# The order of exponentials and probability copies on ScalarE in the steps of NSA attention

## Time and profile before

| what | value |
|---|---|
| runs before | 1071.84 us median of 3 (1071.44 to 1075.18) |
| the profiled execution | 1070.39 us, with a span of 1068.3 us from first to last instruction |
| busy over the span | PE 97%, PEld 81%, DVE 56%, ACT 43%, POOL 12% |
| granted TensorE clock, mean | 0.997 of full speed |
| NSA's steps, from the scores of job 0 to the first product of the next stage | 259.89 to 324.36 us of the span |

### The profile page before, as it was taken

How to read it: one execution, slowest core, us unless ns; L and a number is a source line. 1 busy time by engine, 2 the same in 40 slices (tenths; PEclk the granted TensorE clock), 3 DMA queues, 4 the chain that set the end, 5 groups by cost and what they waited for, 6 DMA issues and landing times.

```text
span 1068.3 us, 13273 instructions
## 1 busy us (share of the span) xinstructions
PE 1033.2 (97%) x5334; PEld 868.8 (81%) x5334; DVE 596.3 (56%) x543; ACT 460.7 (43%) x568; POOL 125.1 (12%) x157
## 2 busy tenths in 40 slices
PE   7999999999999999999999999999997899999997
PEld 6888888889898788898878888888876778888885
DVE  4455543854755754462575544554666884455444
ACT  4555432333773454452434334433436444454430
POOL 1000000232911100000012000000017510000001
PEclk9999999999999999999999999999999999999999
DMA  9656545470311665454447654463522246446531
GB/s 348 220 175 213 206 169 188 138 257 2 110 50 45 234 216 204 166 179 176 158 160 261 218 188 157 158 236 126 209 99 69 90 159 235 157 160 212 179 118 40
DMA packets 78652, 178.51 MB, mean 167 GB/s; under 512 B 2992, under 2 KB 12352, under 8 KB 78608
## 3 DMA queue, kind: packets, MB, share of 16 engines
q1 hardware_dynamic: 76128, 169.16, 45.5%
q0 software_dynamic: 2480, 8.72, 2.5%
HBM read 176.82 MB, written 1.05 MB: 167 GB/s over the span
## 4 chain that ended last, share of the span: by engine, by line
PE 82%; DVE 13%; POOL 3%; ACT 1%; DMA 1%; issue 1%; SPq 0%; POOLq 0%; DVEq 0%; ACTq 0%
PE acc L1193 24%; PE acc L1195 24%; PE acc L1194 24%; DVE w_lo L781 4%; PE trb L1252 4%; PE acc L1396 2%; POOL rstd L480 1%; DVE stats L827 1%; DVE x L835 1%; DVE y L822 1%; PE acc L1375 1%; DMA raw<-ffn_w_gate 1%; DVE neg_max L930 1%; DVE xt_lo L791 1%; PE aux L1445 1%
## 5 line engine op out<-in xcount | busy, mean ns | idle before, releaser
L781 DVE TENSOR_TENSOR w_lo<-raw,w_hi 128x2048 fp32r<-128x2048 f32 (+1 forms) x153 | 348.7, 2283 | 217.4 <-ACT w_hi L575 217.4
L575 ACT ACTIVATE w_hi<-raw 128x2048 fp32r<-128x2048 f32 (+1 forms) x153 | 291.7, 1908 | 259.0 <-PE acc L1195 252.1
L1193 PE MATMUL acc<-w_hi,xt_hi 128*128 128x512 f32 (+1 forms) x992 | 378.8, 382 | 6.0 <-DVE w_lo L781 4.6
L1195 PE MATMUL acc<-w_hi,xt_lo 128*128 128x512 f32 (+1 forms) x992 | 371.9, 375 | 0.0
L1194 PE MATMUL acc<-w_lo,xt_hi 128*128 128x512 f32 (+1 forms) x992 | 371.4, 374 | 0.0
L1193 PEld LDWEIGHTS acc<-w_hi,xt_hi 128*128 128x128 f32 x992 | 186.9, 188 | 41.0 <-DVE w_lo L781 6.5
L1195 PEld LDWEIGHTS acc<-w_hi,xt_lo 128*128 128x128 f32 x992 | 186.7, 188 | 34.2
L1194 PEld LDWEIGHTS acc<-w_lo,xt_hi 128*128 128x128 f32 x992 | 187.1, 189 | 31.4
L1193 PE MATMUL acc<-w_hi,ht_hi 128*128 128x512 f32 x352 | 139.4, 396 | 0.0
L1195 PE MATMUL acc<-w_hi,ht_lo 128*128 128x512 f32 x352 | 138.9, 395 | 0.0
L1194 PE MATMUL acc<-w_lo,ht_hi 128*128 128x512 f32 x352 | 138.9, 395 | 0.0
(11 more groups left out here) (176 smaller groups left out, 735.0 us busy)
## 6 DMA issues: line engine op xcount, KB each, us to landing
raw<-ffn_w_gate SPq DMA_DIRECT2D x44, 1024.0 KB, 5.2
raw<-ffn_w_up SPq DMA_DIRECT2D x44, 1024.0 KB, 5.3
raw<-ffn_w_down SPq DMA_DIRECT2D x44, 1024.0 KB, 5.0
raw<-w_kv SPq DMA_DIRECT2D x8, 1024.0 KB, 5.8
raw<-w_in SPq DMA_DIRECT2D x6, 1024.0 KB, 5.7
raw<-w_out_a SPq DMA_DIRECT2D x4, 1024.0 KB, 7.1
raw<-w_q SPq DMA_DIRECT2D x4, 1024.0 KB, 5.3
raw<-w_out_b SPq DMA_DIRECT2D x4, 1024.0 KB, 4.9
```

Of the source, the lines that this page charges most:

```text
L575: act.activation(w_hi[:, slot, 0:k * c], raw[:, slot, 0:k * c], ACT.Copy).then_inc(hi_ready, 1)
L781: dve.tensor_tensor(w_lo[:, slot, 0:k * c], raw[:, slot, 0:k * c], w_hi[:, slot, 0:k * c].bitcast(F32), ALU.subtract).then_inc(lo_ready, 1)
L1193: pe.matmul(out_ap, s_hi, hi, start=first, stop=False)
L1195: return pe.matmul(out_ap, s_lo, hi, start=False, stop=last)
```

## The change

In each step of NSA attention, ScalarE's exponentials of the newest job come first; the copy of job i-2's transposed probabilities and the copies of the transposed queries follow. The other engines' programs, the semaphores and the counts are as they were.

```diff
             for i, sc, tr, pv in job_steps(NSA_JOBS):
+                if sc:
+                    exps("nsa", NSA_JOBS, i, 0)
                 if tr:
                     copy_p("nsa", i - 2)
                 for part in LATE_PARTS["nsa"].get(i, ()):
                     copy_heads(("qr", "nsa"), 1, part, nqs)
-                if sc:
-                    exps("nsa", NSA_JOBS, i, 0)
                 if i == 1:
                     compressed_exp(1)
                 if i == 3:
```

## The result

The changed kernel took **1084.95 us**, the median of 4 runs (1083.9 to 1086.74), against 1072.82 us for the kernel before in the same comparison (4 runs, 1071.44 to 1075.18): ratio **1.0112**, 95% interval 1.009 to 1.0134. That is 12.1 us slower; 8.4 had been forecast (1080.2, with 1075.5 to 1085.0 as the range).

A forecast was written before the change was run, and what follows sets the result against it. TensorE's own instructions were taken to bound NSA's steps. Seven late copies, 8.03 us, plus 0.4 for plain steps made +8.4 on 1070.39, 1078.8; with 1.45 for the median, 1080.2 us, range 1075.5 to 1085.0.

The forecast's parts named there:

- Nothing is won by earlier exponentials: NSA's steps: TensorE never waits for exponentials, so the gain is put at nothing, not above 0.5 us.
- Seven late places, 8.03 us: Seven NSA steps where a copy behind exponentials reaches TensorE late; the waits add to 8.03 us.
- the wait at pc: Step 3, transposes of the compressed probabilities: they need p0's bank, at 269.87 against 268.38, a wait of 1.49 us.
- T of job 10: Step 12, transposes needing p9's bank: maxima of job 11 come after the second mixing, a wait of 1.50 us.
- The edges and the loading after a wait, 0.4 us: About half of some eight plain steps pay, 0.4 us; weight loading for V bounded by 0 and 0.15 each.
- The clock: Rival: TensorE's clock falls after idling around pc, the next two to four steps slow, 1085 to 1089 us; chance 0.02.
- signs of being right: In the NSA stretch: TensorE busy time still near 62 us, clock 1.00, about 8 us of new idle time.
- Only the clear waits land: Rival: of the late places only the first three cost time, 4.5 us, giving 1076.3 us; chance 0.12.
- plain steps become ScalarE's: Rival: each of tok 1's plain steps pays 0.2 to 0.3 us, 2.5 to 4 in all, 1082 to 1084; chance 0.11.
- not slower: Rival, steps 24 to 26: last exponentials come 0.2 us earlier and every copy is in time, 1071.6 us; chance 0.03.
- small waits (4 to 7): T of job 14 and V of jobs 14, 17 and 21: waits of 1.12, 0.90, 0.70 and 0.83 us.
- The ScalarE rule: Skill-page estimate: exponentials take 0.80 and 1.18 us, not the trace's 0.91 and 1.39, for some 7.1 us; trace preferred.

The follow-up runs named there:

- other_steps: Against the kernel before: exponentials first in 17 steps, copy first in steps 2, 7, 11, 15, 16, 19 and 23; 1075.56 us, ratio 1.0023.
- pool_later: Changed kernel, but GpSimd splits its fourth weight unit only after the second mixing; 1077.41 us in one run.
- all_but_11: Changed kernel, but with the copy first in step 11 alone; 1086.19 us, ratio 1.011 to the kernel before.
- maxima_first: Changed kernel, but VectorE takes the newest job's row maxima ahead of the mixing's last two additions; 1076.44 us, ratio 1.0046 to the kernel before.
- keep_warm: Changed kernel plus 16 idle matmuls on TensorE ahead of the transposes of job 10; 1083.56 us, ratio 1.0105 to the kernel before.
- late_seven: Against the kernel before: exponentials first in steps 2, 7, 11, 15, 16, 19 and 23 alone; 1086.83 us, ratio 1.0137.
- only_11: Against the kernel before: exponentials first in step 11 alone; 1072.86 us, ratio 1.0005.
- mix_early_pool: Kernel before, with part of VectorE's mixing ahead of the row maxima and GpSimd's fourth weight unit split after the second mixing; 1071.04 us, ratio 0.9981.

## Why the prediction was right or wrong

The direction, the places and the mechanism of the waits were right, and the time is inside the range, at its very end. The size fell short: +8.4 was forecast; the medians are 12.1 us apart, and in the profiled executions NSA's steps take 13.6 more, of which 10.2 are waits. That the median lies inside, by 0.05 us, is partly luck: the range had no room for the clock, and how much it fell differs from run to run. By the prediction's own steps:

- *Nothing is won by earlier exponentials.* Right. No kernel here with exponentials first in any step gained, and TensorE never waited for exponentials before. (The one wait for a query copy that the prediction counts into the stretch, 0.34 us, lies just ahead of it.)
- *Seven late places, 8.03 us.* Right in each: forecast 1.49, 1.49, 1.50, 1.12, 0.90, 0.70 and 0.83, measured 1.48, 1.46, 2.43, 0.93, 0.79, 0.63 and 0.76, together 8.48. Six are within 0.2. That the waits simply add is not shown: an eighth place, V of job 2, was 0.86 us late by the same sum and is missing from the list, and it cost only 0.06 us because the wait at pc covered it (other_steps uncovers it). T of job 10 was short by 0.9, since the sum took the maxima at their old place behind the mixing; shifted against GpSimd's splits, the mixing itself got longer. The same adds 0.5 us to the wait for the second mixing (1.21 us by distance of starts, 0.70 before), which the forecast left out. pool_later showed both, 2.2 us with what hangs on them. This term of the sum was mis-sized because VectorE's durations had been taken as fixed when the work beside them moves.
- *The edges and the loading after a wait, 0.4 us.* Too small: what is left of the 10.2 after 8.48 and 0.5 is 1.2 us. About 0.6 is the first matmul after a wait (V takes 1.10 us instead of 1.00 after each of some six waits), the rest waits of 0.04 to 0.18 at the plain steps. Both were bounded rightly and taken at the low end.
- *The clock.* The step that failed: the sum had no term for it, and "the clock 1.00" and "PE's busy time still near 62 us" were named as signs of being right (0.96 and 68.00). It was a rival with a chance of 0.02, dismissed on one wait of 2.28 us at a granted clock of 1.00. It came: half speed for 7 us behind T of job 10, 3.4 us lost, and in all_but_11 and maxima_first, which have the same wait at pc, behind pc with 8.5 us lost: within the 5 to 9 us of that rival and at its place. What sets off a fall stays open: pool_later has the same wait at pc and no fall. One wait without a fall was no evidence that waits are safe. By the Trainium skill, page "TensorE: Matmul & The Clock Gate", section "Part 1: The HAM clock gate", the clock drops to half after idle time; the falls behind the waits of 1.32 and 2.27 us agree with it in kind, the one at 264 us in keep_warm, where TensorE was busy throughout, doesn't follow from it.
- *Only the clear waits land; plain steps become ScalarE's; not slower.* Rightly put low. All four small waits (4 to 7) were there; the plain steps paid 0.6 us in all beside V's longer matmuls, not 2.5 to 4; and all seven copies were late.
- *The ScalarE rule.* By the trace's durations 2.35 us were expected from maxima to TensorE, and 2.37 were measured. By the figures for a single ACTIVATE on the Trainium skill's page "ScalarE: Activation LUTs", section "What ACT_TABLE_LOAD costs", two exponentials were estimated at 0.80 us. They took 0.91 (299.24 to 300.15): the measurement sides with the rows.

## What to carry to other kernels

On an engine that starts its instructions in order, what is ready comes ahead of what has to wait. Here a copy whose input was ready went behind a wait for another engine's result, and it added 10 us although the engine had been idle for over a quarter of the stretch: look at when each product is asked for, not at busy shares. To price such a swap, add up the chain from the late event to the asker (here 2.35 us, right to 0.02 for a transpose and 0.07 for V) and compare it with the asker's start at every step: list the places that an earlier wait covers too, and take extra care at the steps in which the late engine has something else to do. And where a change adds waits on TensorE, leave room in the range for its clock.

## What the runs showed of the hardware

- TensorE's granted clock goes to half speed for stretches in the middle of a busy kernel, in different places from run to run: 7 us behind the wait at T of job 10 (changed kernel and late_seven), 16 us behind the wait at pc (maxima_first and all_but_11), and not at all behind the same wait at pc in pool_later. Much of the spread of this kernel's times goes with it: beside only_11 and mix_early_pool the kernel before took 1069.3 to 1072.0 us at mean clocks of 0.995 and 0.996, and 1076.6 to 1077.0 at 0.987 and 0.988.
- A fall costs nothing where TensorE would have waited anyway: in keep_warm work at half speed up to 269.8 us took the place of the wait of 1.32 us at pc.
- VectorE instructions with two SBUF inputs got longer beside GpSimd's splits, the small ones most: 128x16 elements took 0.17 us with GpSimd still, 0.53 or 1.21 beside it, and 128x512 took 0.69 us, beside it up to 1.66 (all_but_11). Those with an input in PSUM kept their 0.69 us. An engine's duration read from one execution holds for that position against its neighbours only.
- Two complementary halves of an edit need not add up: 74.25 and 68.12 us less clock are 9.8 and 3.65 over the kernel before, together 13.4, where the whole change makes 10.2.
